# Folding the pooling map into the input projection: w_pool multiplied into w_xa once per group, and the pooling products left out

## The reference

```
h = layer_norm(x) * (1 + scale) + shift
xa, ga, u, v, gb = split(h @ w_in)            # each 512 wide
pooled_g = mean of xa_g over the last 2/4/8/16 tokens, minus xa_g    # g = 0..3, 128 channels each
ya_g = (pooled_g @ w_pool[g]) * pool_scale * silu(ga_g)
yb   = gelu(u) * (w_sgu LN(gelu(v)) + b) * silu(gb)
z = alpha * x + gate * (concat(ya, yb) @ w_out);  out = LN(z) * ln_g + ln_b
```

## Time and profile before

| what | value |
|---|---|
| median of 3 runs | 679.13 us (679.03 to 679.43) |
| the profiled execution's own time | 678.93 us |
| its span, first to last instruction | 677.2 us |
| TensorE busy (matmul) | 664.5 us, 98% |
| VectorE busy | 525.6 us, 78% |
| ScalarE busy | 239.3 us, 35% |
| mean granted clock of TensorE | 0.996 |

### The profile page before, as it was taken

One profiled execution on the slowest core, in us unless ns is written; L12 is line 12 of the kernel. 1 busy time (PEld: TensorE's weight loads), 2 busy tenths in 40 slices (PEclk: granted clock), 3 DMA queues, 4 the chain that ended last, 5 costly groups with the idle time before them and its releaser, 6 DMA issues.

```text
span 677.2 us, 8864 instructions
## 1 busy us (share of the span) xinstructions
PE 664.5 (98%) x3087; PEld 552.9 (82%) x3087; DVE 525.6 (78%) x973; ACT 239.3 (35%) x316; POOL 61.9 (9%) x77
## 2 busy tenths in 40 slices
PE   8999999999999999999999999999999999999995
PEld 7888787878888888888888888888888888888884
DVE  5879989859769868759969967776978977555876
ACT  4444434338213333326511333334721333323300
POOL 2000200100012101100002201000002210000010
PEclk9999999999999999999999999999999999999998
DMA  8993352883425442575324362288233463224011
GB/s 332 396 370 131 125 187 88 169 300 129 142 76 186 168 176 93 97 210 223 126 94 155 124 248 93 93 109 324 93 124 123 136 245 117 95 81 162 38 63 62
DMA packets 33976, 106.68 MB, mean 158 GB/s; under 512 B 6509, under 2 KB 7569, under 8 KB 33938
## 3 DMA queue, kind: packets, MB, share of 16 engines
q1 hardware_dynamic: 33938, 106.22, 47.6%
HBM read 97.80 MB, written 8.40 MB: 157 GB/s over the span
## 4 chain that ended last, share of the span: by engine, by line
PE 89%; DVE 5%; issue 3%; ACT 1%; DMA 1%; POOL 0%; SPq 0%; POOLq 0%; DVEq 0%; ACTq 0%
PE bank_b L1008 59%; PE bank_a L1008 26%; PE bank_a L1122 2%; DVE gate_rows L723 1%; DMA x_norm<-in_x 1%; PE bank_b L1068 1%; DVE x_stats L622 1%; PE bank_b L1032 0%; ACT h_high L476 0%; ACT w_high L466 0%; DVE w_low L601 0%; DVE y_low L829 0%; PE bank_b L1087 0%; PE bank_b L1059 0%; DVE mixed L818 0%
## 5 line engine op out<-in xcount | busy, mean ns | idle before, releaser
L1008 PE MATMUL bank_b<-h_high,w_high 128*128 128x512 f32 x512 | 202.1, 395 | 0.6 <-DVE sgu_bias L757 0.6
L1008 PE MATMUL bank_b<-h_low,w_high 128*128 128x512 f32 x512 | 199.4, 390 | 0.0
L1008 PE MATMUL bank_b<-h_high,w_low 128*128 128x512 f32 x512 | 199.4, 389 | 0.0
L466 ACT ACTIVATE w_high<-w_float 128x1024 fp32r<-128x1024 f32 x100 | 105.5, 1056 | 149.5 <-DMA w_float<-in_w_units 56.3
L601 DVE TENSOR_TENSOR w_low<-w_float,w_high 128x1024 fp32r<-128x1024 f32 x100 | 122.1, 1221 | 42.5 <-ACT w_high L466 42.3
L1008 PEld LDWEIGHTS bank_b<-h_high,w_high 128*128 128x128 f32 x512 | 96.2, 188 | 21.0 <-issue 1.8
L1008 PEld LDWEIGHTS bank_b<-h_high,w_low 128*128 128x128 f32 x512 | 96.1, 188 | 20.2
L1008 PEld LDWEIGHTS bank_b<-h_low,w_high 128*128 128x128 f32 x512 | 96.2, 188 | 19.7 <-issue 0.5
L411 POOL TENSOR_TENSOR z_rstd<-z_var_eps,minus_half 128x1 f32<-128x1 f32 x16 | 22.0, 1377 | 367.3 <-DVE z_var_eps L858 357.4
L1008 PE MATMUL bank_a<-w_high,y_high 128*128 128x512 f32 x128 | 49.8, 389 | 0.0
L1008 PE MATMUL bank_a<-w_low,y_high 128*128 128x512 f32 x128 | 49.8, 389 | 0.0
(11 more groups left out here) (180 smaller groups left out, 945.4 us busy)
## 6 DMA issues: line engine op xcount, KB each, us to landing
w_float<-in_w_units SPq DMA_DIRECT2D x104, 512.0 KB, 3.3
x_norm<-in_x SPq DMA_DIRECT2D x16, 512.0 KB, 4.4
z<-in_x SPq DMA_DIRECT2D x16, 512.0 KB, 5.5
out<-z SPq DMA_DIRECT2D x15, 512.0 KB, 4.7
z<-in_mod_units SPq DMA_DIRECT2D x12, 512.0 KB, 9.6
x_norm<-in_x_channels SPq DMA_DIRECT2D x12, 512.0 KB, 13.8
mod_spare<-in_mod_units SPq DMA_DIRECT2D x6, 512.0 KB, 8.2
x_norm<-in_w_units SPq DMA_DIRECT2D x4, 512.0 KB, 4.3
```

Source lines behind the costliest of these rows:

```text
L466: nc.scalar.activation(wH[:, n % S_SLOTS, :], wF[:, n % F_SLOTS, :], ACT.Copy).then_inc(w_high, 1)
L1008: last = mm(bank, wl if n == 2 else wh, ml if n == 1 else mh, start=start and n == 0, stop=stop and n == 2)
```

## The change

Before the change the kernel computes pooled sums and multiplies them by w_pool in every group of every chunk. After it the weights w_xa of each group are multiplied by w_pool once, in chunk 0, and the pooled sums of the new xa are the result.

- `fold_xa(g)`, on TensorE: eight float32 matmuls of 128x128x128 (no split) into two PSUM banks. The stationary operand is a block of unit 4+4g as it landed in its slot of `wF` (the host now stores these units transposed), the moving one is `wpF[:, g]`. It stands behind `early_low_pass(0)` for g = 0, behind unit 6 for g = 1, behind unit 9 for g = 2 and behind unit 13 for g = 3, and waits for the landing of its unit: units 4, 8, 12, 16.
- `fold_copy(g)`, on ScalarE: two copies of 128x512 from PSUM back into the same slot of `wF`, ahead of the unit's split. For g = 0 it stands ahead of `early_high(4)`, and `h_evacuate(0, 1)` has been moved ahead of both.
- `store_xa(g)`, on SP: 512 KB from the slot to `xa_units` in DRAM. The load that uses the slot next (units 2, 10, 14, 18) waits until the store has landed. Chunks 1 to 3 load `xa_units` in place of the xa units.
- w_pool is loaded right behind unit 4 and has a tile of its own; before, it came behind unit 2 and w_sgu.
- Gone are `pool_product`, `pooled_high`, `pooled_low`, `small_weights` and the split of w_pool on ScalarE. `y_pool` reads `S` and runs in the gate's step; for group 0 it stands in `first_branches`, and `y_low` of group 0 at the end of that. `gate_bias` moves from ahead of `sgu_bias` to step n = 15.

```diff
+XA_UNITS = tuple(V_UNITS + 4 * g for g in range(G))
+FOLD_AFTER = {6: 1, 9: 2, 13: 3}
+GATE_BIAS_IN = 15
...
             def load_w(c, n):
                 wait(sp, w_low, c * UNITS + n - F_SLOTS + 1)
+                first = isinstance(c, int) and c == 0 and n < UNITS
+                if first and n - F_SLOTS in XA_UNITS:
+                    sp.wait_ge(xa_stored, (XA_UNITS.index(n - F_SLOTS) + 1) * 16)
+                source = w_units[n % UNITS]
+                if n % UNITS in XA_UNITS and not first:
+                    source = xa_units[XA_UNITS.index(n % UNITS)]
+                sp.dma_start(wF[:, n % F_SLOTS, :], source).then_inc(w_landed[n % F_SLOTS], 16)
+
+            def store_xa(g):
+                sp.wait_ge(fold_copied, g + 1)
+                sp.dma_start(xa_units[g], wF[:, XA_UNITS[g] % F_SLOTS, :]).then_inc(xa_stored, 16)
...
             load_early(4)
+            sp.dma_start(wpF[:, :].rearrange("p (g d) -> p g d", g=G),
+                         w_pool.rearrange("g c d -> c g d")).then_inc(pool_landed, 16)
             load_m(4)
...
             for m in range(8, 12):
                 load_m(m)
+            store_xa(0)
+            sp.wait_ge(xa_stored, 16)
             load_early(2)
...
+            def fold_copy(g):
+                act.wait_ge(folded, g + 1)
+                for half, bank in enumerate(fold_banks(g)):
+                    done = nc.scalar.activation(wF[:, XA_UNITS[g] % F_SLOTS, half * T:(half + 1) * T], bank, ACT.Copy)
+                done.then_inc(fold_copied, 1)
+                act.wait_ge(fold_copied, g + 1)
             early_high(0)
             h_evacuate(0, 0)
+            h_evacuate(0, 1)
+            fold_copy(0)
             early_high(4)
-            h_evacuate(0, 1)
...
             nc.scalar.activation(X[:, HALO:], B[:, 0, :], ACT.Copy).then_inc(xa_copied, 1)
+            fold_copy(1)
             split_high(0, FIRST_LOOP)
...
                 for n in range(FIRST_LOOP if first else 0, IN_UNITS + 1 if last else UNITS):
+                    if first and n + AHEAD in XA_UNITS[2:]:
+                        fold_copy(XA_UNITS.index(n + AHEAD))
                     if not (last and n in LAST_SPLITS_IN):
                         split_high(c, n + AHEAD)
...
             def y_pool(c, g):
-                dve.wait_ge(pool_done, c * G + g + 1)
+                dve.wait_ge(pooled, c * G + g + 1)
                 wait(dve, yp_low, c * G + g)
                 dve.wait_ge(ga_gated, c * G + g + 1)
-                vec.scalar_tensor_tensor(out=yP[:, :], in0=A[:, g % 2, :], scalar=halfc[:, g:g + 1], in1=sga[:, :],
-                                         op0=ALU.mult, op1=ALU.mult).then_inc(yp_ready, 1)
+                vec.scalar_tensor_tensor(out=yP[:, :], in0=S[(g + 1) % 2][:, HALO:], scalar=halfc[:, g:g + 1],
+                                         in1=sga[:, :], op0=ALU.mult, op1=ALU.mult).then_inc(yp_ready, 1)
...
                 pooling(c, 0, True)
                 split_low(c, FIRST_LOOP)
                 v_stats_of(c, 1)
-                pooled_low(c, 0)
                 gate(ga_tanh, ga_gated, sga, 1, 1)
+                y_pool(c, 0)
                 split_low(c, FIRST_LOOP + 1)
...
                 v_norm_of(c, 3)
+                y_low(c, 0, yp_high, yp_low, 0, yP)
...
-            def pool_product(c, g):
-                pe.wait_ge(p_low, c * G + g + 1)
-                pe.wait_ge(v_gelu, (c + 1) * TILES)
-                wait(pe, yp_ready, c * G + g - 1)
-                product(A[:, g % 2, :], wpH[:, g, :], wpL[:, g, :], pH[:, :], pL[:, :],
-                        start=True, stop=True).then_inc(pool_done, 1)
+            def fold_xa(g):
+                slot = XA_UNITS[g] % F_SLOTS
+                if g == 0:
+                    pe.wait_ge(pool_landed, 16)
+                    pe.wait_ge(w_landed[slot], 16)
+                    pe.wait_ge(h_full, 1)
+                else:
+                    pe.wait_ge(w_landed[slot], landed_at(0, XA_UNITS[g]))
+                    pe.wait_ge(v_gelu, TILES)
+                    pe.wait_ge(fold_copied, g)
+                banks = fold_banks(g)
+                for k in range(KT):
+                    cut = slice(k * P, (k + 1) * P)
+                    last = mm(banks[k // 4][:, k % 4 * P:(k % 4 + 1) * P], wF[:, slot, cut],
+                              wpF[:, g * P:(g + 1) * P], start=True, stop=True)
+                last.then_inc(folded, 1)
...
             early_low_pass(0)
+            fold_xa(0)
             early_high_passes(1)
...
             early_channel(u, (7,)).then_inc(unit_done, 1)
+            fold_xa(FOLD_AFTER[V_UNITS + len(EARLY_CHANNEL) - 1])
...
                         if n in sgu_after:
                             sgu_product(c, sgu_after.index(n))
+                        if first and n in FOLD_AFTER:
+                            fold_xa(FOLD_AFTER[n])
```

More of the change, by code:

```diff
@@ L124, in hybrid_layer @@
         wt = sb("w_sgu_turned", [P, G * P])
-        wpH, wpL = sb("w_pool_high", [P, G, P], F32R), sb("w_pool_low", [P, G, P], F32R)
+        wpF = sb("w_pool", [P, G * P])
         E = sb("sgu_bias", [P, G, P])
@@ L251, in early_float, with landed_at, fold_banks @@
             return (wF[:, 0, :], wF[:, 1, :], gateB[:, :], wS[:, :])[EARLY_LANDING[unit]]
+        def landed_at(c, n):
+            early = sum(1 for u in EARLY if EARLY_LANDING[u] == n % F_SLOTS) - len(EARLY) // F_SLOTS
+            return (c * (UNITS // F_SLOTS) + n // F_SLOTS + 1 + early) * 16
+        def fold_banks(g):
+            return (B[:, 0, :], B[:, 1, :]) if g == 0 else (A[:, 0, :], A[:, 1, :])
         def mod_column(k):
@@ L337, in chunk @@
                 for n in range(V_UNITS if first else 0, UNITS):
+                    if first and n + 2 * AHEAD - F_SLOTS in XA_UNITS[1:]:
+                        store_xa(XA_UNITS.index(n + 2 * AHEAD - F_SLOTS))
                     if n + 2 * AHEAD < IN_UNITS + 4 or not last:
@@ L463, in split_high @@
                 wait(act, unit_done, c * UNITS + n - S_SLOTS + 1)
-                before = sum(1 for u in EARLY if EARLY_LANDING[u] == n % F_SLOTS) - len(EARLY) // F_SLOTS
-                act.wait_ge(w_landed[n % F_SLOTS], (c * (UNITS // F_SLOTS) + n // F_SLOTS + 1 + before) * 16)
+                act.wait_ge(w_landed[n % F_SLOTS], landed_at(c, n))
                 nc.scalar.activation(wH[:, n % S_SLOTS, :], wF[:, n % F_SLOTS, :], ACT.Copy).then_inc(w_high, 1)
@@ L525, in _ @@
             nc.scalar.activation(ug[:, :], B[:, 2, :], ACT.Gelu).then_inc(u_gelu, 1)
-            act.wait_ge(pooled, 1)
-            nc.scalar.activation(pH[:, :], S[1][:, HALO:], ACT.Copy).then_inc(p_high, 1)
             split_high(0, FIRST_LOOP + 1)
+            act.wait_ge(yp_ready, 1)
+            nc.scalar.activation(yH[:, 0, :], yP[:, :], ACT.Copy).then_inc(yp_high, 1)
             def chunk(c, first, last):
-                pool_after, sgu_after, mix_in, ys_in = places(first)
+                sgu_after, mix_in, ys_in = places(first)
                 for n in range(FIRST_LOOP if first else 0, IN_UNITS + 1 if last else UNITS):
+                    if first and n + AHEAD in XA_UNITS[2:]:
+                        fold_copy(XA_UNITS.index(n + AHEAD))
                     if not (last and n in LAST_SPLITS_IN):
@@ L741, in _ @@
             gate_sum(1)
-            small_weights()
             h_split(0, 6)
@@ L748, in _ @@
                 gate_sum(k)
-            gate_bias()
             def sgu_bias():
                 dve.wait_ge(e_done, 1)
-                dve.wait_ge(small_high, 1)
+                dve.wait_ge(bias_halved, 1)
                 for h in range(G):
@@ L765, in pooling @@
                     dve.wait_ge(const_ready, 4 + HALO)
-                wait(dve, p_low, c * G + g)
+                wait(dve, yp_ready, c * G + g)
                 wait(dve, h_low, (c + 1) * KT)
@@ L913, in chunk @@
                         if step == 1:
-                            pooled_low(c, g)
-                            wait(dve, yp_ready, c * G + g)
                             gate(ga_tanh, ga_gated, sga, 1, c * G + g + 1)
+                            y_pool(c, g)
                         if step == 3:
-                            if first and g == 0:
-                                dve.wait_ge(small_low, 1)
                             wait(dve, ys_ready, c * G + g)
@@ L936, in chunk @@
                             y_low(c, g, ys_high, ys_low, G + g, mixed)
+                    if first and n == GATE_BIAS_IN:
+                        gate_bias()
                     if last and n in LAST_SPLITS_IN:
@@ L1261, in chunk @@
             def chunk(c, first, last):
-                pool_after, sgu_after, _, _ = places(first)
+                sgu_after, _, _ = places(first)
                 for n in range(V_UNITS + len(EARLY_CHANNEL) if first else 0, IN_UNITS if last else UNITS):
@@ L1280, in chunk @@
                         channel_unit(w, B[:, bank, :]).then_inc(unit_done, 1)
[L1281 to L1284 removed]
```

(6 more changed lines are left out.)

48 lines of the change are left out of this document (12 added, 36 removed).

## The result

The changed kernel takes 682.68 us (median of 16 runs), the kernel before 679.13 (16 runs): a ratio of 1.0048, 95% interval 1.0038 to 1.0057. That is 3.3 us slower by the ratio and 3.55 by the medians; the forecast was 4.4 us slower and 683.5 us. The profiled execution took 682.66 us.

What follows compares the result with a forecast made beforehand. TensorE was taken as the bound nearly everywhere, with other engines near it in chunk 0. 7.1 - 11.2 - 1.0 - 0.56 + 1.7 + 0.35 + 6.2 + 1.8 = +4.4 us on 679.13 gave 683.5 us; range 678.6 to 687.0.

Steps and rivals of the forecast that it cites:

- What is removed: Sixteen pooling products, 48 matmuls, leave TensorE: 11.2 us less, 8.4 of it in chunks 1 to 3.
- What TensorE gets: Four folds of eight float32 matmuls, 1.78 us each, add 7.1 us to TensorE, all in chunk 0.
- Fold 0: Early in chunk 0, TensorE waits 2.1 us for h_split(0, 1), held up behind the fold's copies; net wait 1.7 us.
- rival 4: The clock also falls in the early 2.1 us wait of chunk 0: 1.8 us more, 685.3 us; chance 0.15.
- SP's standstill: SP's queue stands until store_xa(0) lands, about 34 us, holding unit 2 and later loads; priced at 0.
- Rival 3: SP's wait on store_xa(0) starves the first stage: 3 to 5 us more, 686.5 to 688.5 us; chance 0.12.
- the forecast's own signs of being wrong: Wrong if fold 2 begins within 2 us of unit 9's end, or the first 60 us are over 5 us later.
- Fold 2: Behind unit 9 in chunk 0, TensorE stands still 6.2 us for unit 12's load, issued as TensorE arrives.
- Rival 1: Unit 12 lands in the usual time, wait 3.2 us: 680.5 us with clock loss, 678.7 without; chance 0.18.
- The clock at fold 2: The pause ahead of the fold behind unit 9 lowers TensorE's clock afterwards: 1.8 us more.
- Fold 3 and the other waits: From the fold behind unit 13 on, splits, stores (4.7 us each) and gate_bias make TensorE wait for nothing: 0.

Runs made afterwards that it cites:

- fold2_late: The changed kernel with the fold of group 2 moved from behind unit 9 to behind unit 10: 680.17 us, ratio 1.0033 to the kernel before.
- the filled pause: The changed kernel with unread matmuls of constants, 8 ahead of the low pass and 14 ahead of the fold of group 2: 679.5 us, ratio 1.0016.
- gate_first: both_moved with ScalarE's copies of chunk 0's gate rows ahead of the split of unit 21: 675.25 us, ratio 0.9948 to the kernel before.
- both_moved: The changed kernel with the moves of fold2_late and hsplit_first together: 677.77 us, ratio 0.9988 to the kernel before.
- no_folds: The changed kernel without folds, their copies and stores, w_pool left out of the result, for timing only: 670.49 us, ratio 0.9879 to the kernel before.
- hsplit_first: The changed kernel with h_split(0, 1) put ahead of early_low(4) on VectorE in chunk 0: 679.95 us, ratio 1.0015 to the kernel before.

## Why the prediction was right, point by point

- **What is removed** held: 8.35 us of 8.4 in chunks 1 to 3, and TensorE stayed the bound there. (The "four places" at which TensorE waited are four lines of the list and six waits; nothing hangs on it.)
- **What TensorE gets** held: 1.78 to 1.80 us for a fold at full clock, 2.04 where TensorE had just waited 0.25 us, 2.97 for the one in which the clock fell. That w_xa is folded first also cost nothing by its loads.
- **Fold 0** held in mechanism and size: the low pass waited 1.9 us for 2.1, the chain through two copies, early_high(4), early_low(4) and h_split is in the trace. The clock, which the forecast kept at 1.00 there and gave to rival 4 with 0.15, fell in the profiled execution and cost some 1.6 us (3.15 for 1.78 and 0.71 for 0.45). In the trace of `fold2_late` the same wait of 1.9 us was not followed by a fall.
- **SP's standstill** held: the store landed 10.4 us after its issue at 23.45, unit 2 was issued at 33.86, and nothing on TensorE waited for what stood behind it. Rival 3 is out. Yet one of the forecast's own signs of being wrong was met by a hair, the first 60 us over 5 us later: the product at 54.23 before stands at 59.38 after, 5.15 us later, by the low clock of rival 4 and not by the queue.

```profile
54.23 0.70 PE bank_b L1008 x3
```

```profile
59.38 0.70 PE bank_b L1026 x3
```

- **Fold 2** is the term that was mis-sized: forecast 6.2 us of wait, measured 3.2. The place and the cause held to 2 us, as did the coincidence of both paths: the load was issued at 91.89, TensorE ran dry at 91.9. The step that failed is "the same four transfers follow each other now. So TensorE stands still for 6.2 us": a single landing of one trace was taken for the rule, against the median of all loads, and its length put down to the four transfers close together. Nine traces with the same four transfers show 3.1 to 3.3 us; the five long ones had a transfer on an instruction queue beside them. Rival 1 had the right size for it, with 0.18.
- **The clock at fold 2** held: 2.97 instead of 1.78 and 6.19 instead of 5.46, 1.9 us for 1.8. Some 0.3 of it is the start behind a wait: against the filled pause it is 1.6.
- **Fold 3 and the other waits** were priced at 0 and cost 0.45 us. The stores of folds 1 to 3, put at 4.7 us, landed in 2.6. In the trace the split of unit 19 stands behind `gate_bias` (1.21 us at 133.84) and the held split of unit 16, the load of unit 21 went out at 142.11, 18.8 us ahead of unit 20 where it had been 20.0 before, and ScalarE had the gate rows behind its split. That these two are what made it late is read from the order in the trace; `gate_first` shows only that the copies' place made the wait.

So the total is near, to 1 us, in part by luck: 3.0 us too much at fold 2 and 1.6 + 0.45 too little elsewhere largely cancel. What the runs show for sure is that the direction hung on the order of the steps around the folds. With fold 2 one unit later and two lines exchanged the change is level with the kernel before (ratio 0.9988), and with the gate rows' copies moved too it is faster, 675.25 us, 0.52% less.

## What to carry to other kernels

A product folded into weights is paid once, but at the busiest moment: ask on which engine queue each fold, copy and store stands and who is behind it. Here the order cost 6 to 7 us, twice what the arithmetic left as a gain in the end. When TensorE gets less to do, work out anew what was just in time for it: 3 us of slack at the gate rows became waits of 0.45 to 2.8 us in five of the kernels that left their copies in place. And do not price a transfer by one landing; take the median and the extremes, and see what else was on the way at the time, on the queues of the kind "instruction" too. A second trace of the same kernel would not have told here: it had the long landing too.

## What the runs showed of the hardware

A pause of TensorE of 1.9 us was followed by the 1.2 GHz clock in one trace (the changed kernel) and not in another (`fold2_late`). One of 2.8 us (`both_moved`) was not, while those of 2.6 (`no_folds`), 3.2 (the changed kernel) and 3.3 (`hsplit_first`) were. In the changed kernel the fall came 0.9 and 1.4 us after the work had resumed. It makes executions of one kernel differ: 678.2 to 685.0 us in ten with pauses of 1.9 and 1.3 us (`fold2_late`), 678.5 to 680.4 in eleven with the pauses filled, 674.9 to 675.6 in five with none over 0.5 us behind the first load (`gate_first`). A 512 KB load behind 2 MB took 16.4 us to land, alone 3.2. A store of 512 KB to DRAM landed in 2.6 us in a quiet queue and in 10.4 in a full one. Loads of 512 KB into an idle queue took at most 3.8 us, 493 of them, unless a 16 KB transfer on a queue of the kind "instruction" fell into their flight; then 27 of 70 took longer, up to 6.3.
